# Delta net's inverse on Trainium2: the squares of the untransposed power on the other two tiles of TensorE

## What is computed

```python
n_mat = -jnp.where(strict, jnp.einsum('bhncd,bhnkd->bhnck', kbeta, kc) * decay, 0.0)
t_mat = jnp.eye(CHUNK, dtype=f32) + n_mat
power = n_mat
for _ in range(int(math.log2(CHUNK)) - 1):
    power = power @ power
    t_mat = t_mat + t_mat @ power
u = t_mat @ (vc * bc[..., None])
w = t_mat @ (kbeta * jnp.exp(gc)[..., None])
```

## Time and profile before

| | |
|---|---|
| median of 3 runs | 2106.27 us |
| span of the profiled execution | 2106.5 us |
| TensorE matmuls (PE) busy | 1783.3 us, 85% |
| weight loads (PEld) busy | 1289.2 us |
| DVE (VectorE) busy | 900.1 us, 43% |
| ACT (ScalarE) busy | 671.8 us, 32% |
| POOL (GpSimd) busy | 195.5 us, 9% |

### The profile page before, as it was taken

How to read it: one execution, slowest core, us unless ns; L and a number is a source line. 1 busy time by engine, 2 the same in 40 slices (tenths; PEclk the granted TensorE clock), 3 DMA queues, 4 the chain that set the end, 5 groups by cost and what they waited for, 6 DMA issues and landing times.

```text
span 2106.5 us, 40152 instructions
## 1 busy us (share of the span) xinstructions
PE 1783.3 (85%) x16826; PEld 1289.2 (61%) x16827; DVE 900.1 (43%) x1454; ACT 671.8 (32%) x890; POOL 195.5 (9%) x169
## 2 busy tenths in 40 slices
PE   6999999999999999999977676676666666676699
PEld 6788888888788888888754333333333334333377
DVE  4665555665464454445343222222222222222274
ACT  4366655566563434333321100010001101011073
POOL 3433333333100000000000000000000000000000
PEclk9999999999999999999989899899999888988899
DMA  8655555454446555568769999999999999999962
GB/s 173 161 136 140 139 139 138 120 134 126 139 160 200 184 196 192 188 198 302 266 274 425 425 425 426 425 427 424 425 426 428 426 427 424 427 427 426 420 239 83
DMA packets 258922, 593.14 MB, mean 282 GB/s; under 512 B 31530, under 2 KB 171050, under 8 KB 225322
## 3 DMA queue, kind: packets, MB, share of 16 engines
q1 hardware_dynamic: 258858, 592.19, 75.4%
HBM read 590.07 MB, written 2.10 MB: 281 GB/s over the span
## 4 chain that ended last, share of the span: by engine, by line
PE 57%; DMA 37%; issue 2%; ACT 1%; DVE 1%; DVEq 0%; POOL 0%; SPq 0%; ACTq 0%; POOLq 0%
DMA ring<-in_w_e_down 37%; PE bank L739 22%; PE bank L560 11%; PE bank L563 6%; PE bank L930 4%; PE bank L993 4%; PE bank L903 1%; PE bank L642 1%; ACT ring L1047 1%; PE bank L649 0%; ACT wh L1047 0%; PE bank L889 0%; PE bank L580 0%; PE bank L878 0%; PE bank L536 0%
## 5 line engine op out<-in xcount | busy, mean ns | idle before, releaser
L1047 ACT ACTIVATE wh<-ring 128x2048 fp32r<-128x2048 f32 x156 | 297.3, 1913 | 212.9 <-DMA ring<-in_w_in 100.8
L903 PE MATMUL bank<-ring,mo 128*32 128x128 f32 x6144 | 212.0, 297 | 134.7 <-DMA ring<-in_w_e_up 115.1
L903 PEld LDWEIGHTS bank<-ring,mo 128*32 128x32 f32 x6144 | 184.8, 120 | 176.8 <-DMA ring<-in_w_e_up 143.3
L1601 DVE TENSOR_TENSOR wl<-ring,wh 128x2048 fp32r<-128x2048 f32 x86 | 197.0, 2291 | 211.5 <-ACT wh L1047 211.5
L560 PE MATMUL bank<-xhl,wh 128*128 128x512 f32 x1024 | 278.0, 410 | 0.0
L1047 ACT ACTIVATE mo<-bank 128x128 f32<-128x128 f32 (+5 forms) x208 | 64.0, 315 | 655.2 <-PE bank L917 306.1
L930 PE MATMUL bank<-ring,mo 128*32 128x512 f32 x1024 | 163.0, 769 | 90.9 <-DMA ring<-in_w_e_down 85.7
L560 PEld LDWEIGHTS bank<-xhl,wh 128*128 128x128 f32 x1024 | 183.8, 188 | 40.2 <-issue 5.3
L469 POOL TENSOR_TENSOR wl<-ring,wh 128x512 fp32r<-128x512 f32 x132 | 175.2, 1359 | 324.1 <-ACT wh L1047 324.1
L739 PE MATMUL bank<-wh,xhl 128*128 128x512 f32 x768 | 186.4, 392 | 0.4 <-DVE mo L1422 0.4
L739 PEld LDWEIGHTS bank<-wh,xhl 128*128 128x128 f32 x768 | 143.3, 188 | 30.8 <-DVE mo L1422 0.8
(11 more groups left out here) (355 smaller groups left out, 2136.6 us busy)
## 6 DMA issues: line engine op xcount, KB each, us to landing
ring<-in_w_e_down SPq DMA_DIRECT2D x64, 2048.0 KB, 26.3
ring<-in_w_e_up SPq DMA_DIRECT2D x64, 2048.0 KB, 26.5
ring<-in_w_in SPq DMA_DIRECT2D x116, 1024.0 KB, 5.5
ring<-in_w_e_gate SPq DMA_DIRECT2D x32, 2048.0 KB, 30.7
xnT<-in_w_e_gate SPq DMA_DIRECT2D x16, 2048.0 KB, 29.7
mo<-in_w_e_gate SPq DMA_DIRECT2D x16, 2048.0 KB, 34.1
ring<-in_w_out SPq DMA_DIRECT2D x16, 1024.0 KB, 5.2
ring<-in_w_ple_gate SPq DMA_DIRECT2D x8, 2048.0 KB, 14.7
```

Of the source, the lines that this page charges most:

```text
L903: m = mm(bank[b][32 * j:32 * j + 32, 0:P], xw[:, 8 * (i % 2) + k, :], m_gu[piece][:, k, j * P:j * P + P], start=(i % 2 == 0 and k == 0), s ...
L1047: return act.activation(out, in_, func, **kw)
L1601: tt(ul[u % PAIRS], unit_slot[u % PAIRS], uh[u % PAIRS], ALU.subtract).then_inc(sem("u_lo"), 1)
```

## The change

The squares of round r (r < 5) move ahead of the products, `t` by `t`, and write the other half of the partitions: rows 0 to 63 to partitions 64 to 127, and the reverse. ScalarE's one copy of 128 partitions becomes two of 64, which swap the halves back. `dn_sqr` is raised by the last product now.

```diff
                     for t in range(TT):
                         for i, rows_ in enumerate(BLOCKS):
+                            if r < 5:
+                                w_ = powT[rows_, t, 0, :] if r else nT[rows_, t, CH * i:CH * i + CH]
+                                mm(pm_psum[BLOCKS[1 - i], t, :], w_, pm[rows_, t, :], start=True, stop=True)
+                        for i, rows_ in enumerate(BLOCKS):
                             if r == 0:
                                 m_ = mm(pow_psum[rows_, t, 0, :], pm[rows_, t, :], nT[rows_, t, CH * i:CH * i + CH],
                                         start=True, stop=True)
...
-                    if r < 5:
-                        for t in range(TT):
-                            for i, rows_ in enumerate(BLOCKS):
-                                w_ = powT[rows_, t, 0, :] if r else nT[rows_, t, CH * i:CH * i + CH]
-                                m_ = mm(pm_psum[rows_, t, :], w_, pm[rows_, t, :], start=True, stop=True)
                     m_.then_inc(sem("dn_sqr"), 1)
...
                 for r in range(5):
                     act.wait_ge(*event("dn_sqr", 6 * n - 5 + r))
-                    f(pm, pm_psum, ACT.Copy).then_inc(sem("dn_roundp"), 1)
+                    f(pm[BLOCKS[0], :, :], pm_psum[BLOCKS[1], :, :], ACT.Copy)
+                    f(pm[BLOCKS[1], :, :], pm_psum[BLOCKS[0], :, :], ACT.Copy).then_inc(sem("dn_roundp"), 1)
```

## The result

The change takes 2099.91 us (median of 6 runs, 2097.45 to 2103.79) against 2106.28 us before (6 runs, 2103.55 to 2109.45): ratio 0.9969, 95% interval 0.9960 to 0.9979, so 4.4 to 8.4 us less. Forecast were 5.0 us less, 2101.3 us, and a range from 2100.0 to 2106.8. One later execution of the kernel before took 3431.28 us, in a slow state; no ratio counts it.

A forecast was written before the change was run, and what follows sets the result against it. TensorE's issue was taken to bound the head stage; seven heads keeping 0.56 us and the eighth 1.06 gave 5.0 us, so 2106.27 - 5.0 = 2101.3 us, range 2100.0 to 2106.8.

The forecast's parts named there:

- What bounds: Head stage, 110 to 590 us: TensorE busy 477.55 of 480 us, so time gained there should reach the end whole.
- What the change does to a round: On TensorE squares lie beside products: rounds 1 to 4 fall from 0.81 to 0.60 us, round 0 from 0.61 to 0.39.
- rival 2: On TensorE the squares wait for the products' rows; a round stays 0.81 us, total 2106.3 us; chance 0.15.
- rival 1: On TensorE matmuls start in order, so overlap is partial; a round gains 0.15 us, total 3.8 us; chance 0.13.
- What it runs into: Before rounds 2 and 3 of seven heads TensorE newly waits for DVE; those heads keep 0.56 us, the eighth 1.06.
- The lid: DVE's taps between rounds limit seven heads: TensorE can start round 2 only 0.09 us early, round 3 0.14.
- ScalarE: The squares' copy becomes two crossed ones; the second adds 0.21 us, 8.4 us in all, and hides.
- The rule of the Trainium skill: On TensorE a weight load overlaps running matmuls only on another row group; would expose loads at three tile-set changes per round.
- Rival 3: In the head stage DVE does not hold TensorE back; all 8.5 us arrive, 2097.8 us; chance 0.05.
- Rival 4: Changing tile set empties TensorE's array, 0.09 us each, 10.8 us slower, 2117.1 us; chance 0.12 including exposed loads.
- How the numbers follow: For the whole kernel: full overlap with DVE's lid, 4.3 to 5.3 us, chance 0.55; time 2101.3, range 2100.0 to 2106.8.
- The chances: For the whole kernel's time: faster by over 0.2% 0.51, slower 0.12, within 0.2% 0.37.

The follow-up runs named there:

- e2: The change with the squares on the other two tiles and crossed copies, but left behind the products in program order: 2098.02 us, ratio 0.9971 to before.
- e5: The change with the next head's four convolution taps one round later on DVE, behind rounds 1 to 4: 2096.67 us, ratio 0.9958 to before.
- e6: The kernel before with the next head's convolution taps one round later on DVE: 2104.65 us, ratio 1.0003 to before.
- e8: The change without the convolution taps between the rounds, one multiplication standing in, so its output differs: 2096.10 us, ratio 0.9957 to before.
- e1: The change run again unaltered, eight runs: 2098.62 us, ratio 0.9972 to before.
- e4: The change with convolution tap 0 on DVE written as scalar-tensor-tensor, adding a zero column: 2101.86 us, ratio 0.9986 to before.

## Why the prediction was right and where it was wrong

- **What bounds.** Right: the stage is as long as TensorE's stream, and its 5.4 us arrive at the end.
- **What the change does to a round.** Right to 0.01 us: 0.60 and 0.39. The assumption that all four tiles run at once holds in the trace; rival 2 (pairs in a row, 0.81) falls, and so does rival 1 (matmuls start in program order, 0.75): by the 0.60, and by e2's starts.
- **What it runs into.** Right: the new waits for DVE are there, ahead of rounds 2 and 3, in the seven heads with taps, and e5, e6 and e8 show that they are the whole of what is missing. The lid's size was off a little: a head keeps 0.61 us instead of 0.56. Counted from round 0, round 2 starts 0.07 to 0.09 us earlier than before (predicted 0.09) and round 3 0.14 to 0.17 (predicted 0.14); rounds 3 and 4 then give 0.217 each and not 0.21, and some 0.02 behind them were not traced. The eighth keeps 1.17 instead of 1.06, of which 1.09 are its rounds; the other 0.08 were not traced. In the stage this makes 7 x 0.61 + 1.17 = 5.4 instead of 5.0.
- **ScalarE.** Right that it hides. A second copy costs 0.28 us, not 0.21: the pair takes 0.56.
- **The rule of the Trainium skill** on weight loads (TensorE: Matmul & The Clock Gate, Part 3) does not hold here: the products' loads begin at 138.31, 0.01 us behind the squares on the same rows, whose next pass on that tile starts only at 138.41, and the products' matmuls begin at 138.31 too.
- **Rival 3** (no lid, 8.5 us) was right in its size, and wrong for this kernel: it is what e5 and e8 do.
- **Rival 4** (a change of tile set empties the array) falls: L640 of the second block and L643 of the first have different rows and the same output partitions, in two banks, and start 0.01 us apart. What costs 0.09 us between L665 and L667 is therefore not the change of rows by itself; whether it is the transposition or the shared bank was not tried.
- **How the numbers follow.** Here lies the step that failed: terms of the gain were too small, and with them the low end of the range. The sum had a head keep 0.56 us (measured 0.61) and the eighth 1.06 (1.17), 5.0 in all where the stage gave 5.4. Its far end, 5.3, for which the prediction shows no working, was passed too. "1.0 us more because the lid is read from one head" was added to it and gave 2100.0; the measured 2099.91 lies 0.09 below. Of the 6.4 us between the medians, the other 1.0 has no place in the kernel that a trace shows: the spread outside the stage is larger (e1), and e1's own medians lie 6.1 apart. The prediction had no term for that spread. The three runs it was made from agreed within 0.7 us, while later executions of the same kernel go from 2101.3 to 2109.6, and the interval of the measured gain is 2 us wide on each side. On which side of 2100.0 the time fell is therefore chance; that the gain was put too low is not. The forecast itself, 5.0, lies in the measured interval (4.4 to 8.4).
- **The chances.** Faster by over 0.2% got 0.51 and came true, by little: 0.31%, with an interval from 0.21 to 0.40%, and 0.26% by the stage's 5.4 us. The lid brings the gain near that line; e5, without it, has 0.42%.

## What to carry to other kernels

Small matmuls of 64 rows by 64 columns leave half of TensorE idle when both kinds sit on the two diagonal tiles; put the second kind on the other two (output on the other half of the partitions; here the two kinds also write different banks, and no run shows what one bank would do) and let the engine that copies it out swap the halves back, which costs one more copy and nothing for the crossing. The order in the program need not be changed for that; but as starts no longer follow it, make sure that whatever raises the semaphore comes last (in e2 the signal came after the products all the same). When a stage gets shorter, look first at the engine that was ready only just in time: here TensorE could start round 2 less than 0.1 us and round 3 about 0.15 us earlier before it met DVE. No list of waits shows that, and it took 3.3 of 8.7 us until DVE's own work was moved one round later.

## What the runs showed that was not expected

- Matmuls on different tiles start independently of program order: in e2 passes of L649 start at 135.85 between those of L642, although six more of L642 stand ahead of them (135.99, 136.10). The semaphore that the last L649 raises still came 0.38 us behind the start of the last product.
- DVE's tensor-scalar on 128x256 fp32 in SBUF takes 1.3 us beside GpSimd's 128x512 subtractions and 0.34 to 0.35 us without (e5, e8); with the zero column added (e4), beside them, 1.4 to 1.5 us. The copy of 12 columns took 0.16 us in the change, where it began 0.09 us before GpSimd's work, and 1.12 us in e5, where it fell in the middle of it. Not every instruction slows: the sum L1548, which reads a bank, takes 0.28 us beside GpSimd (140.90) as behind it (143.11).
- Two 64-partition copies by ScalarE take 0.56 us, crossed or not.
